# Weight sums of a Strassen-Winograd layer: six slabs in heads 0 to 6, their copies begun by GpSimd

## The chip, the cores and the metric

The kernel is one program on one core of a Trainium2 chip. The metric is the device time of one execution in microseconds (us). The shown time is the median of three runs.

## The reference, cut to what matters

One decoder layer over 512 tokens of width 2048, in float32. A combined projection feeds two branches of eight heads each, a gated delta rule and block attention. Their outputs are projected up, gated, summed, projected by `w_o` and added to the input.

```python
h = rms_norm(x, norm_w)                       # 512 x 2048
proj = h @ w_in                               # heads' q, k, v, z of both branches, and the gates
oa = gated_delta_rule(...) ; ob = moba_attention(...)
y_gdn, y_moba = oa @ w_out_gdn, ob @ w_out_moba
merged = sigmoid(g_gdn) * y_gdn + sigmoid(g_moba) * y_moba
out = x + merged @ w_o
```

## The kernel before

**Stages.** First the input is normalised and transposed. Then eight heads follow (`head(h, p)` on every engine; heads 1 to 6 are a loop). A head multiplies eight windows of `w_in`, each a block of 2048 x 128 weights (1 MB), with the tokens: the "windows" w = 0 to 7, named `win(w, ...)` on TensorE (PE). Between their pieces TensorE does the small products of the delta rule of head h and of the attention of the head before, p. After the heads come ten "quads", `q` = 0 to 9: 0 to 3 form the gates, 4 to 7 the two up-projections, 8 and 9 the product with `w_o`. A quad is a product of 2 x 2 blocks done with seven block products instead of eight (P11, P12, PS1, PS2, PS4, PS3, P22), each split in units, and for that sums of weight blocks are needed.

**A weight's way.** The sync engine (SP) loads window w into one of four slots (`load`, line 547), once the window that used the slot is done. ScalarE (ACT) rounds it (`split`, line 1386), VectorE (DVE) forms the rest (line 1840), and TensorE multiplies three times (lines 885 to 889). ACT and DVE do this in the order written: a weight that is late holds whatever stands behind its split. In the order of ACT, behind the split of window 1 stand the gate of z, the rounded rotary outputs and the evacuation of window 0 (line 1418); behind the split of window 2 stands the SiLU of head h (lines 1394 to 1398), which leads over DVE lines 1883 and 1887 to TensorE's line 935.

**Weight sums.** `w_out_gdn`, `w_out_moba` and `w_o` need four sums of blocks each, T1 to T4. They are built in DRAM (`weight_sums`) by DMAs alone, in eight slabs of rows, one slab for each head. A slab has 64, 64 and 128 rows of the three weights. It takes 12 plain copies, issued by SP between its weight loads (`sum_copies`, line 554; one or two behind each load), six accumulating DMAs from the weights (`sums_13`, lines 764 and 766), three that add T3 to T2 (`sums_2`, line 772) and three that add T2 to T4 (`sums_4`, line 779). The accumulating ones are issued by GpSimd (POOL), for the slab of the head before. The slabs of heads 6 and 7 are summed by GpSimd in quads 1 and 2, between its stores of the gates. The sums are read from quad 4 on.

**GpSimd's order in a head.** It makes the decay parts (lines 747 to 758), loads the next decay row (742), stores the attention output of the head before (795), issues `sums_13`, does the rotary product of k (`k_rope`, 811), issues `sums_2`, does the rotary product of q (`q_rope`, 811), stores the delta rule's output (815) and issues `sums_4`.

**GpSimd's order in a gate quad.** `add_22` (line 839) adds a weight block to an operand, and `finish_block` (line 847) stores a block of gates to DRAM. ACT may overwrite a block buffer (`e_block`, line 1724) only once its store has landed. Between these stand, in quads 1 and 2:

```python
                for i in range(3):
                    finish_block(q, i)
                    if q in (1, 2):
                        (sums_13, sums_2, sums_4)[i](last - 2 + q)
```

Of the kernel before, what the change touches and what calls it, by code (L numbers as in the profile page):

```python
# [18 lines left out]
H = 8  # L19
# [16 lines left out]
NW = len(STRIPES)  # L36
# [6 lines left out]
COLS = 512  # L43
# [36 lines left out]
def ended(q, p):  # L80
    return unit(q, p, ku(q) - 1) + 1
# [113 lines left out]
T_FIRST = ((0, 0), (0, 0), (0, 1), (1, 0))  # L195
T_OF = {PS1: T1, PS2: T2, PS3: T3, P22: T4}
NT_COPIES = 12
PAIRED = P // 2

(HC_G, HC_CG, HC_B, HC_NB, HC_NBE, HC_KD, HC_GL) = range(7)  # L200
NHC = 7
RING = 4
# [23 lines left out]
def hybrid_layer(nc, x, norm_w, w_in, gdn_conv_w, gdn_a_log, gdn_dt_bias, gdn_norm_w, moba_q_norm_w,  # L226
# [11 lines left out]
    t_dram = [nc.dram_tensor(f"weight_sums{i}", (4, rows, 2, COLS), F32, kind="Internal").ap()  # L238
              for i, rows in enumerate((D // 4, D // 4, D // 2))]
    w_blocks = [w[0].rearrange("(b r) (q s c) -> b r q s c", b=2, q=2, s=2) for w in (w_out_gdn, w_out_moba, w_o)]  # L240
# [3 lines left out]
    with ctx:  # L244
        def sb(name, shape, dt=F32, at=ctx):
            return at.enter_context(nc.sbuf_tensor(name, shape, dt))

        s = {n: ctx.enter_context(nc.semaphore(n)) for n in SEMS}
# [66 lines left out]
        masked4 = sb("masked4", [P, P], at=area)  # L315
        pairs4 = sb("pairs", [P, 4, PAIRED], at=area)
        steps = sb("level_rows", [P, PAIRED], at=area)
        area.close()
# [63 lines left out]
        def compact(ap, rows):  # L382

            return ap[:rows, :NT * PAIRED]

# [89 lines left out]
        def weight_sum(q, t, j):  # L475

            of, at = (2, q - W0) if q >= W0 else ((q - Y0) // 2, q % 2)
            return t_dram[of][t, UK * j * P:UK * (j + 1) * P, at, :].rearrange("(k p) c -> p k c", p=P)

        def slab(of, t, i):  # L480

            r = t_dram[of].shape[1] // H
            return t_dram[of][t, bass.ds(i * r, r), :, :]

        def block_slab(of, kb, cb, i):

            r = t_dram[of].shape[1] // H
            return w_blocks[of][kb, bass.ds(i * r, r), :, cb, :]

        residual = ops[:, SLOT_C, 2, :].rearrange("p (t c) -> p t c", t=2)  # L490

# [35 lines left out]
        def _(sp):  # L527
# [19 lines left out]
                sp.dma_start(raw[slot][:].rearrange("p (k c) -> p k c", k=src.shape[1]), src)\  # L547
                    .then_inc(loaded[slot], 16)

            def sum_copies(i, w):  # L550

                for c in range(w, NT_COPIES, NW):
                    of, t = c % 3, c // 3
                    sp.dma_start(slab(of, t, i), block_slab(of, *T_FIRST[t], i)).then_inc(s["wt_copied"], 16)

            def head_loads(i):
                sp.wait_ge(s["wt_copied"], 16 * NT_COPIES * i)
                for w, (_, col) in enumerate(STRIPES):
                    if w == 0:
                        slot_free(i * NW + 1)  # L560
                    elif w > 1:
                        slot_free(i * NW + w)
                    load(i * NW + w, w % RING, w_in3[:, :, bass.ds(i * P + col, P)])
                    sum_copies(i, w)

            load(0, 0, w_in3[:, :, STRIPES[0][1]:STRIPES[0][1] + P])
            sp.wait_ge(s["sets"], 1)
# [11 lines left out]
            for w in range(RING, NW):  # L579
                slot_free(w)  # L580
                load(w, w % RING, w_in3[:, :, STRIPES[w][1]:STRIPES[w][1] + P])
                for c in range(w - RING, NW, RING):
                    sum_copies(0, c)
            with sp.Fori(1, H) as i:
                head_loads(i)

# [81 lines left out]
            def stream():  # L668

                gate_after = {}  # L670
                for b in range(GATES, 4 * (W0 - Y0)):
                    q, i = Y0 + (b - GATES) // 4, (b - GATES) % 4
                    gate_after[ended(q, BLOCK_PRODUCT[i]) + LEAD + NSTREAM] = (Y0 + b // 4, b % 4)
                sp.wait_ge(s["wt_sums"], 16 * NT_COPIES * H)
                for n in range(unit(Y0), N_UNITS):
                    if n == unit(Y0) + NSTREAM - 1:
                        sp.wait_ge(s["pe_unit"], ended(Y0 - 1, PS4))
                        sp.wait_ge(s["ob_out"], 16 * H)
                        sp.dma_start(stage(1), o_dram[H:].rearrange("k p t -> p k t")).then_inc(s["stage_b"], 16)
                    load_streamed(n)  # L680
                    if n == unit(Y0) + NSTREAM:
                        for b in range(GATES):
                            load_gate(Y0, b)
                    if n in gate_after:
                        load_gate(*gate_after[n])
# [30 lines left out]
        def _(pool):  # L716
# [27 lines left out]
            def decay_parts(h):  # L744
# [12 lines left out]
                pool.wait_ge(s["cg_dts"], 4 * h + 2)  # L757
                pool.tensor_tensor(dTb[:], dTb[:], nb_row, ALU.mult).then_inc(s["cg_dts"], 1)

            def sums_13(i):  # L760

                pool.wait_ge(s["wt_copied"], 16 * NT_COPIES * (i + 1))
                for of in range(3):
                    pool.dma_start(slab(of, T3, i), block_slab(of, 1, 1, i), accum_op=ALU.add).then_inc(s["wt_sums"], 16)
                for of in range(3):
                    pool.dma_start(slab(of, T1, i), block_slab(of, 0, 1, i), accum_op=ALU.add).then_inc(s["wt_sums"], 16)

            def sums_2(i):

                pool.wait_ge(s["wt_sums"], 16 * (NT_COPIES * i + 6))  # L770
                for of in range(3):
                    pool.dma_start(slab(of, T2, i), slab(of, T3, i), accum_op=ALU.add,
                                   max_dma_last_dim=4 * 2 * COLS).then_inc(s["wt_sums"], 16)

            def sums_4(i):

                pool.wait_ge(s["wt_sums"], 16 * (NT_COPIES * i + 9))
                for of in range(3):
                    pool.dma_start(slab(of, T4, i), slab(of, T2, i), accum_op=ALU.add,
                                   max_dma_last_dim=4 * 2 * COLS).then_inc(s["wt_sums"], 16)  # L780

            def head(h, p):

                decay_parts(h)
                if p is None:
                    store_rows()
                if h is not last:
                    decay_row(h + 1)
                if h is last:
                    store_own(0, 0)  # L790
                    store_own(0, 1)
                    store_own(1, 0)
                if p is not None:
                    pool.wait_ge(s["ob"], h)
                    pool.dma_start(o_dram[bass.ds(p + H, 1)].rearrange("o p t -> p (o t)"), pr1[:])\
                        .then_inc(s["ob_out"], 16)
                    if h is not last:
                        sums_13(p)

                if h is last:  # L800
                    store_own(1, 1)
                    store_own(2, 0)
                    store_own(2, 1)
                pool.wait_ge(s["rope_loaded"], 16)
                for c, r in ((0, kr), (1, qr)):
                    if h is last and c == 1:
                        store_own(3, 0)
                        store_own(3, 1)
                    pool.wait_ge(s["b_n"], 2 * h + c + 1)
                    pool.wait_ge(s["s_mm"], 4 * h)  # L810
                    pool.tensor_tensor(r[:], pt[:, c, :], cos, ALU.mult).then_inc(s["b_cos"], 1)
                    if c == 0 and p is not None and h is not last:
                        sums_2(p)
                pool.wait_ge(s["o_2"], h + 1)
                pool.dma_start(o_dram[bass.ds(h, 1)].rearrange("o p t -> p (o t)"), o1[:]).then_inc(s["o_out"], 16)
                if p is not None and h is not last:
                    sums_4(p)

            last = H - 1
# [4 lines left out]
                pool.wait_ge(s["a_step"], own_count(OWN_LAST[i], half))  # L824
                pool.dma_start(own_dram[i][:, k], own[:, k]).then_inc(own_stored[half], 16)

            head(0, None)
            with pool.Fori(1, H - 1) as i:
                head(i, i - 1)
            head(last, last - 1)  # L830

# [29 lines left out]
            for q in range(NQ):  # L862
                if q < Y0:
                    add_22(q, 0)
                    add_22(q, 1)
                if q > 0:
                    finish_block(q - 1, 3)
                if q < Y0:
                    add_22(q, 2)
                    add_22(q, 3)  # L870
                for i in range(3):
                    finish_block(q, i)
                    if q in (1, 2):
                        (sums_13, sums_2, sums_4)[i](last - 2 + q)
            for i in range(4):
                pool.wait_ge(e_stored[i], stored(LAST if i < 3 else LAST - 1))

# [2 lines left out]
        def _(pe):  # L880
# [92 lines left out]
            def ma(h, k):  # L973
# [6 lines left out]
                if k == NL - 1:  # L980
                    for t in range(NT):
                        mm = pe.matmul(G0[:LAST_ROWS, t * PAIRED:(t + 1) * PAIRED], Ln[:, t * P:t * P + LAST_ROWS],
                                       xa[:, tile4h(t)[1]], start=True, stop=True)
                else:
                    m = P - b
                    for t in range(NT):
                        mm = pe.matmul(G0[:m, t * PAIRED:(t + 1) * PAIRED], Ln[:, t * P:t * P + m],  # L987
                                       half_tile(xa, t, b, 1), start=True, stop=True)
# [1589 lines left out]
```

## Time and profile before

| | us |
|---|---|
| median of 3 runs | 1577.79 |
| lowest, highest | 1574.37, 1577.83 |
| the profiled execution's own time | 1578.1 |
| its span in the profile | 1576.5 |
| TensorE busy | 1535.1 (97%) |
| VectorE, ScalarE, GpSimd busy | 1064.0, 766.4, 251.4 |

The profile lists busy time by engine, what ended each idle stretch, and the DMA queues: the queue `hardware_dynamic` takes what SP issues, `software_dynamic` what GpSimd issues. An engine that is rarely idle bounds the kernel; idle time elsewhere costs nothing by itself. Timelines give each instruction's start and length in us, and in brackets the idle time before it and what ended it. TensorE's instructions overlap, so its pace is read from the distance of their starts.

### The profile page before, as it was taken

To read this page: it belongs to the slowest core of one execution; us is meant where nothing else is said; L and a number is where in the kernel's file an instruction comes from. 1 tells how busy PE (TensorE), PEld (TensorE's weight loads), DVE (VectorE), ACT (ScalarE), POOL (GpSimd) and SP (SyncE) were. 2 spreads that over 40 slices of the span, in tenths; PEclk is the share of its full clock that TensorE was granted. 3 is DMA by queue.
4 is the path that set the end of the run, shared out by engine and by line. 5 is a ranking of instruction groups with operands and counts; after the bars stand their busy time and mean duration, and the time that the engine had idled before them with its cause. 6 is when DMAs were issued, how large, how long until landed. Compare 5 with 4: busy or idle time off the path is not lost.

```text
span 1576.5 us, 20948 instructions
## 1 busy us (share of the span) xinstructions
PE 1535.1 (97%) x7591; PEld 1285.3 (82%) x7591; DVE 1064.0 (67%) x1331; ACT 766.4 (49%) x1007; POOL 251.4 (16%) x253
## 2 busy tenths in 40 slices
PE   6999999999999999999999999999797999999998
PEld 5888888888888888888888888887686888888887
DVE  6665756746757557657578879685674898767744
ACT  5434434335344344344344456655473775556542
POOL 4202023023112121140230101112021000100000
PEclk9999999999999999999999999999898999999999
DMA  8426369288376575493593467679598688986864
GB/s 271 142 87 201 106 123 258 75 183 222 95 194 175 121 191 168 99 245 114 108 257 115 147 233 179 193 236 248 139 254 194 224 281 306 310 258 206 255 207 107
DMA packets 236320, 296.74 MB, mean 188 GB/s; under 512 B 11299, under 2 KB 143654, under 8 KB 235174
## 3 DMA queue, kind: packets, MB, share of 16 engines
q1 hardware_dynamic: 208006, 221.46, 44.8%
q0 software_dynamic: 28256, 74.49, 22.5%
q8 instruction: 37, 0.61, 0.2%
q14 instruction: 21, 0.17, 0.0%
HBM read 270.72 MB, written 96.50 MB: 233 GB/s over the span
## 4 chain that ended last, share of the span: by engine, by line
PE 88%; DMA 7%; DVE 2%; ACT 1%; POOL 1%; issue 1%; SPq 0%; ACTq 0%; DVEq 0%
PE bank L885 15%; PE bank L889 15%; PE bank L887 14%; PE bank L1326 10%; PE bank L1328 10%; PE bank L1330 10%; DMA weight_sums<-in_w_o_dram 3%; PE bank L914 2%; DMA gates<-e_block 2%; PE bank L987 1%; PE bank L1004 1%; DMA weight_sums<-weight_sums 1%; PE bank L1081 1%; PE bank L919 1%; DMA x_tiles<-in_x_dram 1%
## 5 line engine op out<-in xcount | busy, mean ns | idle before, releaser
L885 PE MATMUL bank<-h_hi_r,w_hi 128*128 128x512 f32 x1008 | 407.4, 404 | 0.0
L889 PE MATMUL bank<-h_hi_r,w_raw_r 128*128 128x512 f32 x1008 | 394.6, 391 | 0.0
L887 PE MATMUL bank<-h_lo_r,w_hi 128*128 128x512 f32 x1008 | 393.6, 390 | 0.0
L2341 DVE TENSOR_TENSOR ring_lo<-operands,ring_hi 128x1024 fp32r<-128x1024 f32 x224 | 271.1, 1221 | 166.6 <-ACT ring_hi L1683 165.0
L1683 ACT ACTIVATE ring_hi<-operands 128x1024 fp32r<-128x1024 f32 x224 | 235.3, 1059 | 209.5 <-PE bank L1330 190.6
L889 PEld LDWEIGHTS bank<-h_hi_r,w_raw_r 128*128 128x128 f32 x1008 | 189.2, 188 | 41.5
L887 PEld LDWEIGHTS bank<-h_lo_r,w_hi 128*128 128x128 f32 x1008 | 189.9, 188 | 34.7
L885 PEld LDWEIGHTS bank<-h_hi_r,w_hi 128*128 128x128 f32 x1008 | 189.8, 188 | 34.1
L1326 PE MATMUL bank<-ring_hi,h_hi_r 128*128 128x512 f32 x480 | 188.5, 393 | 0.2 <-issue 0.2
L1328 PE MATMUL bank<-ring_lo,h_hi_r 128*128 128x512 f32 x480 | 186.8, 389 | 0.0
L1840 DVE TENSOR_TENSOR w_raw_r<-w_raw,w_hi 128x2048 fp32r<-128x2048 f32 x64 | 151.2, 2363 | 32.1 <-ACT w_hi L1386 31.0
L1330 PE MATMUL bank<-ring_hi,h_lo_r 128*128 128x512 f32 x416 | 161.9, 389 | 0.0
L1330 PE MATMUL bank<-ring_hi,sums_r 128*128 128x512 f32 x384 | 151.5, 394 | 0.0
L1326 PE MATMUL bank<-ring_hi,sums_r 128*128 128x512 f32 x320 | 127.8, 399 | 20.6 <-DVE ring_lo L2341 20.6
L1328 PE MATMUL bank<-ring_lo,sums_r 128*128 128x512 f32 x320 | 126.7, 396 | 0.0
L1386 ACT ACTIVATE w_hi<-w_raw 128x2048 fp32r<-128x2048 f32 x64 | 122.1, 1908 | 0.0
L1326 PEld LDWEIGHTS bank<-ring_hi,h_hi_r 128*128 128x128 f32 x480 | 90.1, 188 | 19.4 <-issue 0.8
L1328 PEld LDWEIGHTS bank<-ring_lo,h_hi_r 128*128 128x128 f32 x480 | 90.1, 188 | 18.7 <-issue 0.2
L1330 PEld LDWEIGHTS bank<-ring_hi,h_lo_r 128*128 128x128 f32 x416 | 78.1, 188 | 16.3
L1326 PEld LDWEIGHTS bank<-ring_hi,sums_r 128*128 128x128 f32 x320 | 61.4, 192 | 34.8 <-issue 21.1
L1330 PEld LDWEIGHTS bank<-ring_hi,sums_r 128*128 128x128 f32 x384 | 73.4, 191 | 15.7
L1328 PEld LDWEIGHTS bank<-ring_lo,sums_r 128*128 128x128 f32 x320 | 61.5, 192 | 12.7
(327 smaller groups left out, 2172.0 us busy)
## 6 DMA issues: line engine op xcount, KB each, us to landing
w_raw<-in_w_in_dram SPq DMA_DIRECT2D x64, 1024.0 KB, 7.5
operands<-in_w_in_dram SPq DMA_DIRECT2D x64, 512.0 KB, 5.7
operands<-weight_sums SPq DMA_DIRECT2D x64, 512.0 KB, 5.3
weight_sums<-in_w_o_dram SPq DMA_DIRECT2D x32, 512.0 KB, 6.2
operands<-in_w_o_dram SPq DMA_DIRECT2D x24, 512.0 KB, 5.0
weight_sums<-in_w_out_gdn_dram SPq DMA_DIRECT2D x32, 256.0 KB, 6.3
weight_sums<-in_w_out_moba_dram SPq DMA_DIRECT2D x32, 256.0 KB, 7.5
weight_sums<-in_w_o_dram POOLq DMA_DIRECT2D x16, 512.0 KB, 13.5
```

The lines of the kernel that those rows point to most:

```text
L885: pe.matmul(PJ[slot % 2][:], w_hi[slot % 2][:, c], h_hi[:, k, :], start=(k == 0), stop=False, skip_group_check=True)
L887: pe.matmul(PJ[slot % 2][:], w_hi[slot % 2][:, c], h_lo[:, k, :], start=False, stop=False, skip_group_check=True)
L889: mm = pe.matmul(PJ[slot % 2][:], w_lo[slot][:, c], h_hi[:, k, :], start=False, stop=(k == KT - 1), skip_group_check=True)
L914: mm = pe.matmul(ps[:, tile4(t)], lhsT[:, tile4(t)], rhs[:, tile4(t)], start=True, stop=True)
L919: mm = pe.transpose(ps[:, tile4(t)], src[:, tile4(t)], ident[:])
L1326: pe.matmul(ps[:], a_hi, ring_hi[:, n % RINGS, c], start=(FRESH[p] and k == 0), stop=False, skip_group_check=True)
L1328: pe.matmul(ps[:], a_hi, ring_lo[:, n % RINGS, c], start=False, stop=False, skip_group_check=True)
L1330: mm = pe.matmul(ps[:], a_lo, ring_hi[:, n % RINGS, c], start=False, stop=(k == kn - 1), skip_group_check=True)
L1386: act.activation(w_hi[slot % 2][:], raw[slot][:], ACT.Copy).then_inc(s["hi_ready"], 1)
L1683: act.activation(ring_hi[:, n % RINGS, :], operand(q, p, j), ACT.Copy).then_inc(s["op_hi"], 1)
L1840: dve.tensor_tensor(w_lo[slot][:], raw[slot][:], w_hi[slot % 2][:].bitcast(F32), ALU.subtract)\
L2341: dve.tensor_tensor(ring_lo[:, n % RINGS, :], operand(q, p, j), ring_hi[:, n % RINGS, :].bitcast(F32), ALU.subtract).then_inc(s["op_lo"], 1)
```

## The change

The sums are built in six slabs instead of eight. Each but the last has 88, 88 and 176 rows; the last (slab 5) has 72, 72 and 144. The twelve copies of slab i are issued by GpSimd in head i, for i = 0 to 5: six behind the rotary product of k (and behind `sums_2`, where there is one), six behind the rotary product of q. SP issues no copies and no longer waits for them at a head's start. `sums_13`, `sums_2` and `sums_4` of slab i are issued in head i + 1, so all is done in heads 0 to 6; quads 1 and 2 have no sums. The accumulating DMAs between sums are cut into pieces of half the length.

```diff
+SLABS = H - 2
+LAST_SLAB = SLABS - 1
...
+        def slab_rows(of, i):
+
+            n = t_dram[of].shape[1]
+            r = 8 * -(-n // (8 * SLABS))
+            if i is LAST_SLAB:
+                return slice(i * r, n)
+            return bass.ds(i * r, r)
...
-            def sum_copies(i, w):
-
-                for c in range(w, NT_COPIES, NW):
-                    of, t = c % 3, c // 3
-                    sp.dma_start(slab(of, t, i), block_slab(of, *T_FIRST[t], i)).then_inc(s["wt_copied"], 16)
...
             def head_loads(i):
-                sp.wait_ge(s["wt_copied"], 16 * NT_COPIES * i)
...
                     load(i * NW + w, w % RING, w_in3[:, :, bass.ds(i * P + col, P)])
-                    sum_copies(i, w)
...
+            def sum_copies(i, first):
+
+                for t in (first, first + 1):
+                    for of in range(3):
+                        pool.dma_start(slab(of, t, i), block_slab(of, *T_FIRST[t], i)).then_inc(s["wt_copied"], 16)
...
-                                   max_dma_last_dim=4 * 2 * COLS).then_inc(s["wt_sums"], 16)
+                                   max_dma_last_dim=2 * 2 * COLS).then_inc(s["wt_sums"], 16)
...
-            def head(h, p):
+            def head(h, p, copied=None):
...
                     if c == 0 and p is not None and h is not last:
                         sums_2(p)
+                    if copied is not None:
+                        sum_copies(copied, 2 * c)
...
-            head(0, None)
-            with pool.Fori(1, H - 1) as i:
-                head(i, i - 1)
+            head(0, None, 0)
+            with pool.Fori(1, LAST_SLAB) as i:
+                head(i, i - 1, i)
+            head(LAST_SLAB, LAST_SLAB - 1, LAST_SLAB)
+            head(SLABS, LAST_SLAB)
             head(last, last - 1)
...
-                    if q in (1, 2):
-                        (sums_13, sums_2, sums_4)[i](last - 2 + q)
```

## Rows read from the trace of the kernel before

**Rows 1.** The page: busy time by engine, and its share.
```profile
PE 1535.1 (97%) x7591; PEld 1285.3 (82%) x7591; DVE 1064.0 (67%) x1331; ACT 766.4 (49%) x1007; POOL 251.4 (16%) x253
```

**Rows 2.** Windows: one head, quad 1, quad 3; granted clock, DMA share, GB/s last.
```profile
501.00:612.00 111.00, 111.00 (x582) 93.75 (x581) 70.13 (x106) 48.07 (x72) 22.26 (x21) 1.00 0.64 161
1048.00:1138.00 90.00, 79.61 (x340) 65.30 (x339) 55.01 (x53) 45.48 (x49) 17.73 (x20) 0.92 0.82 212
1228.00:1315.00 87.00, 87.00 (x386) 72.03 (x385) 75.11 (x76) 62.32 (x70) 4.36 (x8) 1.00 0.82 284
```

**Rows 3.** Chain of work across the end of quad 1: start, us, what.
```profile
1083.27 9.81 DMA weight_sums<-weight_sums
...
1096.41 12.90 DMA gates<-e_block
```

**Rows 4.** TensorE's timeline at the starts of quads 2 and 3.
```profile
1112.82 0.76 PE L1326 MATMUL bank<-ring_hi,sums_r 128*128 128x512 f32 x1 [10.39 <-DVE ring_lo L2341]
...
1118.93 0.40 PE L1330 MATMUL bank<-ring_hi,sums_r 128*128 128x512 f32 x1
1119.16 0.40 PE L1326 MATMUL bank<-ring_hi,sums_r 128*128 128x512 f32 x1
...
1201.99 0.77 PE L1326 MATMUL bank<-ring_hi,sums_r 128*128 128x512 f32 x1 [9.88 <-DVE ring_lo L2341]
```

**Rows 5.** ScalarE's timeline at the start of quad 1.
```profile
1022.02 1.09 ACT L1724 ACTIVATE e_block<-bank 128x512 f32<-128x512 f32 x2 [5.52 <-DMA gates<-e_block]
```

**Rows 6.** GpSimd's timeline, end of head 4 and start of head 5.
```profile
560.95 2.44 POOL L772 DMA_DIRECT2D weight_sums<-weight_sums  x3
578.86 1.79 POOL L811 TENSOR_TENSOR q_rope<-pt,cossin 128x512 f32<-128x512 f32 x1 [15.46 <-DVE pt L2031]
...
588.46 1.04 POOL L747 TENSOR_TENSOR lower<-lower,hcol 128x512 f32<-128x512 f32 x1 [1.24 <-ACT lower L1434]
```

**Rows 7.** The sync engine's timeline there: the loads of windows 0 and 2.
```profile
564.01 0.38 SPq L547 DMA_DIRECT2D w_raw<-in_w_in_dram  x1
...
577.54 0.38 SPq L547 DMA_DIRECT2D w_raw<-in_w_in_dram  x1
```

**Rows 8.** DMA issues: the loads issued at 564.01, 625.42 and 646.00; last is us to landing.
```profile
w_raw<-in_w_in_dram SPq DMA_DIRECT2D x1, 1024.0 KB, 9.5
...
w_raw<-in_w_in_dram SPq DMA_DIRECT2D x1, 1024.0 KB, 6.2
...
w_raw<-in_w_in_dram SPq DMA_DIRECT2D x1, 1024.0 KB, 13.9
```

**Rows 9.** DMA queues, 652 to 656: packets, MB, share of 16 engines.
```profile
q0 software_dynamic: 355, 0.66, 89.3%
q1 hardware_dynamic: 358, 0.19, 22.9%
```

**Rows 10.** DMA packets in 628 to 631, 674 to 678, and 683 to 685.
```profile
DMA packets 1632, 0.95 MB, mean 316 GB/s; under 512 B 17, under 2 KB 1554, under 8 KB 1632
...
DMA packets 217, 0.76 MB, mean 189 GB/s; under 512 B 32, under 2 KB 32, under 8 KB 217
...
DMA packets 675, 0.77 MB, mean 385 GB/s; under 512 B 31, under 2 KB 389, under 8 KB 675
```

**Rows 11.** ScalarE's timeline, the splits of windows 0, 1 and 2 of head 5.
```profile
581.15 1.90 ACT L1386 ACTIVATE w_hi<-w_raw 128x2048 fp32r<-128x2048 f32 x1
...
589.25 1.91 ACT L1386 ACTIVATE w_hi<-w_raw 128x2048 fp32r<-128x2048 f32 x1
...
600.13 1.91 ACT L1386 ACTIVATE w_hi<-w_raw 128x2048 fp32r<-128x2048 f32 x1
```

**Rows 12.** VectorE's timeline behind the split of window 2.
```profile
603.98 2.29 DVE L1840 TENSOR_TENSOR w_raw_r<-w_raw,w_hi 128x2048 fp32r<-128x2048 f32 x1
...
608.29 0.69 DVE L1887 TENSOR_TENSOR raw_gk_r<-raw_gk,out_norm_r 128x512 fp32r<-128x512 f32 x1 [1.42 <-ACT out_norm_r L1447]
```

**Rows 13.** TensorE's timeline, the product that waits for it.
```profile
612.36 0.39 PE L935 MATMUL bank<-out_norm_r,ones 128*128 128x512 f32 x1
```

More of the change, by code:

```diff
@@ L478, in weight_sum @@
             return t_dram[of][t, UK * j * P:UK * (j + 1) * P, at, :].rearrange("(k p) c -> p k c", p=P)
+        def slab_rows(of, i):
[4 more added lines that the diff above has]
+            return bass.ds(i * r, r)
         def slab(of, t, i):
-            r = t_dram[of].shape[1] // H
-            return t_dram[of][t, bass.ds(i * r, r), :, :]
+            return t_dram[of][t, slab_rows(of, i), :, :]
         def block_slab(of, kb, cb, i):
-            r = t_dram[of].shape[1] // H
-            return w_blocks[of][kb, bass.ds(i * r, r), :, cb, :]
+            return w_blocks[of][kb, slab_rows(of, i), :, cb, :]
         residual = ops[:, SLOT_C, 2, :].rearrange("p (t c) -> p t c", t=2)
@@ L581, in _ @@
                 load(w, w % RING, w_in3[:, :, STRIPES[w][1]:STRIPES[w][1] + P])
-                for c in range(w - RING, NW, RING):
-                    sum_copies(0, c)
             with sp.Fori(1, H) as i:
@@ L673, in stream @@
                     gate_after[ended(q, BLOCK_PRODUCT[i]) + LEAD + NSTREAM] = (Y0 + b // 4, b % 4)
-                sp.wait_ge(s["wt_sums"], 16 * NT_COPIES * H)
+                sp.wait_ge(s["wt_sums"], 16 * NT_COPIES * SLABS)
                 for n in range(unit(Y0), N_UNITS):
@@ L779, in sums_4 @@
                     pool.dma_start(slab(of, T4, i), slab(of, T2, i), accum_op=ALU.add,
-                                   max_dma_last_dim=4 * 2 * COLS).then_inc(s["wt_sums"], 16)
-            def head(h, p):
+                                   max_dma_last_dim=2 * 2 * COLS).then_inc(s["wt_sums"], 16)
+            def head(h, p, copied=None):
                 decay_parts(h)
```

## The prediction

> **What bounds the kernel now.** First the page: TensorE is busy for 97% of the span [rows 1], so only what makes it wait, run at a lower clock or do other work counts; the change leaves its work alone. Then the windows by stage: in the head stage TensorE is never idle, with the DMA engines busy for 0.64 of the time; in quad 3 it is never idle either; in quad 1 it is busy for 79.6 of 90 us and its mean clock is 0.92 [rows 2]. Quad 2 repeats quad 1.
>
> Then TensorE's timeline: it stands still for 10.39 us where quad 2 begins and for 9.88 us where quad 3 begins [rows 4]. The chain of work says for what: GpSimd waits for a DMA between sums (9.81 us), then stores the last gates of the quad, and this store takes 12.90 us to land [rows 3]; only then may ScalarE empty the bank. So the stalls come from sums standing in GpSimd's order ahead of a gate store, and from their bytes in the same DMA engines. After a stall the distance of matmul starts is 0.43 us and not 0.23: the 14 steps from 1112.82 to 1118.93 take 6.11 us instead of 3.2 [rows 4], the 1.2 GHz level instead of the 2.4.
>
> **What the removal in quads 1 and 2 gives.** Idle 10.39 + 9.88 = 20.3 us, plus 2.9 us of low clock twice, is 26 us. What is late next: the same store without sums ahead of it. The trace has this case at the start of quad 1: ScalarE waits 5.52 us for the gates, until 1022.02 [rows 5], and TensorE does not wait. Shifted by a quad (76.2 us, which is 336 matmuls of 0.227) this gives 1098.2 for the start of quad 2, against 1109.4 now, 11.2 us earlier and so 0.8 more than the stall: just enough. I take the full 26 us; the lower bound is half of it, if one of the two stays.
>
> **What the heads pay: GpSimd's order.** Three DMAs hold GpSimd for 2.44 us [rows 6], so six copies take 4.9. Those behind k's product and `sums_2` end near 568.5; q's product starts at 578.86 after 15.46 us idle [rows 6], so 10 us are spare. Those behind q's product end near 585.6; behind them wait the store of the delta rule's output (0.6 us), `sums_4` (2.4) and the decay parts, which start at 588.46 now [rows 6] and then near 588.7 or a us later. VectorE reads them behind its line 1887, at 608.29 [rows 12], when they have been done for over 10 us. Price nothing. SP loses waits that hid nothing: its loads start when a slot is free [rows 7].
>
> **What the heads pay: the DMA engines.** Now a copy stands in SP's queue behind a load and can't delay it. Then the copies are in GpSimd's queue, beside the loads. From 652 to 656 both queues had work, a load beside accumulating sums, and moved 355 and 358 packets [rows 9]: they take turns packet by packet, though one's are 2 KB and the other's 512 B. That load took 13.9 us to land, one alone 6.2 [rows 8]. (By the Trainium skill, DMA: Bandwidth & Descriptors, Queues, rings and completion order, each engine goes round the queues packet by packet; the trace agrees.)
>
> Price of a packet on one of 16 engines: a load's 512 B, 48 / 1632 = 0.03 us; a 4 KB piece of `sums_2`, 64 / 185 = 0.346; a copy's 2 KB, by 385 GB/s over 16, 0.085 [rows 10]. A GpSimd copy is not in the trace. Its bounds are 0.07 (the same window, loads taken out) and 0.161 (an accumulating 2 KB packet, 64 x 0.893 / 355 [rows 9]). I take 0.085, since SP's plain copies are of the same blocks.
>
> Per engine a load has 128 packets, `sums_2` 22 (16 x 1.375), each half of the copies 2 x (11 + 11 + 22) = 88, `sums_4` 22. Walk through the end of head 4 with the times of [rows 6, 7], a first packet 1.6 us after an issue (4 for GpSimd's copies, an estimate) and 0.6 from the last packet to landing:
> - Load 0, issued 564.01, starts at 565.6. `sums_2` has 13 packets left: 13 x 0.376 = 4.9, to 570.5. Then 88 turns of 0.115 beside copies, 10.1, to 580.6; 27 left alone, 0.8. Lands 582.0 (now 573.5 [rows 8]).
> - Load 1, queued behind, runs alone until the second six copies begin at 584.7, then 18 turns beside them. Lands 587.4.
> - Load 2, issued 577.54, meets 70 copies (8.1 us, to 594.9), the store (0.8) and all of `sums_4` (22 x 0.376 = 8.3, to 604.0), then 32 alone. Lands 605.6 instead of about 585.
>
> The limits. TensorE reaches window 2 nine matmuls before 612.36 [rows 13], so at 610.3, window 1 at 599.4, window 0 at 588.5. A weight needs 1.9 us of ScalarE [rows 11] and 2.3 of VectorE [rows 12] first. So load 0 must land by 584.3, load 1 by 594.5, load 2 by 606.1. Behind the split of window 2 stands one more thing: line 1887 ends at 608.98 [rows 12], 3.4 us before its product at 612.36 [rows 13]; VectorE's split may begin at 607.4 instead of 603.98, so load 2 must land by 605.5. By the walk it is 0.1 us late, with nothing to spare. Slabs of 88 rows don't divide by 16, so some engines carry more than 88 packets; each extra one costs 0.115, and a load lands with its last engine. I add 1.4 us: 1.5 us lost in a head.
>
> This meets the heads that have `sums_2`, copies and `sums_4`, 1 to 5: 5 x 1.5 = 7.5 us. In head 0 there are no sums (15 us less traffic): nothing. Head 6 has sums alone: nothing. `sums_13` grows from 64 to 88 packets, 24 x 0.161 = 4 us, beside the load of window 7, which has 20 us of cover: nothing.
>
> **Sum.** 1578.1 - 26 + 7.5 = 1559.6 on the profiled execution, whose own time is 0.3 above the median: 1559.5.
>
> **Rivals.**
> - *The loads come too late (slower).* Place: load 1 and load 2 at a head's start. Both sets of 88 copies lie ahead of load 2, so each 0.01 us on a copy's packet costs 1.8 us a head. From 0.114 us a packet on, the loss passes 26 / 5 = 5.2 us a head and the kernel is slower. At 0.13, load 2 is 8 us late, 40 in all: 1592. At 0.161, load 0 lands at 588.7 and load 1, which meets all 88 later copies and `sums_4`, at 615, 20 us late: 1650. For it: turns by packet, the DMA share of 0.64 over a whole head already [rows 2]. Against it: SP's copies at 385 GB/s. Chance 0.22.
> - *Uneven engines.* If the 88-row transfers all lie on the same eleven engines, those carry 108 copies and 32 pieces of sums: 2 x (20 x 0.115 + 10 x 0.376) = 12 us later for load 2, 1612. The Trainium skill (same page, Why a DMA increments its semaphore by 16 and not by 1) says that a DMA uses the largest number up to 16 that divides its slowest dimension, 11 for 88 rows, from a cursor that moves on for GpSimd's. No row here shows a size that doesn't divide by 16. With the cursor the excess is a few packets, which my 1.4 us covers. Its chance is within the 0.22.
> - *No price at all.* A packet at 0.07 lands load 2 at 603: 1552. Chance 0.10.
> - *The gain is only moved.* The gate stores of quads 1 and 2 stay late by DMA load alone, and one stall remains: 1572. Against it: quad 3, as loaded with DMA (0.82) and never idle [rows 2]. Chance 0.05.
> - *GpSimd blocks* on copies that find no room behind queued ones, until they drain at 581: q's product 2 us late, then VectorE and its split of window 0, which has 3 us spare. With it the time is above 1565. Chance 0.03.
>
> **How the numbers follow.** My forecast, 0 to 4 us lost a head, 1553 to 1573, has 0.54; no price 0.10; slower 0.22; what is left, 0.06, is a loss near 5 us a head, no change. A measurement of this kernel tells about 0.3%, 4.7 us. The moved gain and the block end faster. Faster 0.71, same 0.07, slower 0.22. The range reaches from the case of no price, 1551, into the slow rival, 1600, leaving out what lies beyond a packet of 0.14; the likeliest case's own is 1553 to 1573.
>
> **What would show it.** Right: no wait of TensorE above 1 us at the starts of quads 2 and 3, clock 1.00 in quad 1, gate stores landing in 7 to 9 us; in the heads, the loads of windows 0, 1 and 2 landing near 18, 23 and 28 us after issue, q's product and the decay parts on time; TensorE idle 0 to 4 us about 24 us into a head (line 935 or window 2). Wrong: loads landing in 8 to 10 us (then the queues share otherwise than by turns), TensorE idle at windows 0 or 1 of a head, a period of a head above 116 us with lower clock behind the stall, or copies' packets at other than 0.07 to 0.1 us.

## The result, and the profile after

| | before | after |
|---|---|---|
| median of 6 runs, us | 1575.86 | 1615.24 |
| lowest, highest | 1574.37, 1577.83 | 1610.74, 1618.6 |
| span of the profiled execution | 1576.5 | 1617.0 |
| TensorE busy | 1535.1 | 1542.0 |

The ratio is 1.0246, 95% interval 1.0225 to 1.0268: slower, where 1559.5 and faster had been forecast. It is outside the range (1551 to 1600) too. Ratios, here and below, compare undisturbed executions alone; one of E10 (5492 us) and one of E12 (2194 us), far off all others, are in no ratio, but the medians listed for these two runs count them.

The page of the kernel after: busy time by engine, granted clock in 40 slices, and the loads (the last figure is the median us to landing).

```profile
PE 1542.0 (95%) x7591; PEld 1289.2 (80%) x7591; DVE 1055.3 (65%) x1331; ACT 765.5 (47%) x1007; POOL 264.8 (16%) x301
...
PEclk9999998998998998999999999999999999999999
...
w_raw<-in_w_in_dram SPq DMA_DIRECT2D x64, 1024.0 KB, 9.7
```

The list of TensorE's waits: us in all, times, the longest. L889 is the first product of every window, so its line adds the waits of all windows.

```profile
PE bank L889 <- DVE w_raw_r L1844: 54.3, 6, 12.5
PE bank L1258 <- DVE x_tiles L2243: 11.1, 1, 11.1
PE bank L1330 <- DVE ring_lo L2345: 0.8, 1, 0.8
```

Windows of the kernel after: the end of head 4, the 12.5 us behind its stall, and quad 1; clock, DMA share, GB/s last [rows 2].

```profile
533.00:644.50 111.50, 100.03 (x533) 84.33 (x532) 62.80 (x100) 41.50 (x63) 22.38 (x28) 0.97 0.64 160
644.50:657.00 12.50, 12.50 (x49) 10.22 (x50) 5.25 (x6) 6.00 (x9) 5.45 (x5) 0.88 0.95 253
1079.00:1166.00 87.00, 87.00 (x386) 72.04 (x385) 58.71 (x56) 50.06 (x54) 12.49 (x13) 1.00 0.72 214
```

The quads are as forecast: no stall left that counts, clock 1.00 in quad 1, where it was 0.92 [rows 2, 4]. The time was lost in the heads, where the forecast had lost 1.5 us each. TensorE's timeline has a stall at the start of each of heads 2 to 6, at the first product of window 0 (the sixth wait of L889, 1.6 us, is at window 1 of head 6):

```profile
267.37 0.79 PE L889 MATMUL bank<-h_hi_r,w_hi 128*128 128x512 f32 x1 [11.61 <-DVE w_raw_r L1844]
...
393.06 0.79 PE L889 MATMUL bank<-h_hi_r,w_hi 128*128 128x512 f32 x1 [12.26 <-DVE w_raw_r L1844]
...
519.24 0.79 PE L889 MATMUL bank<-h_hi_r,w_hi 128*128 128x512 f32 x1 [12.45 <-DVE w_raw_r L1844]
...
644.47 0.79 PE L889 MATMUL bank<-h_hi_r,w_hi 128*128 128x512 f32 x1 [11.47 <-DVE w_raw_r L1844]
645.06 0.63 PE L891 MATMUL bank<-h_lo_r,w_hi 128*128 128x512 f32 x1
645.49 0.63 PE L893 MATMUL bank<-h_hi_r,w_raw_r 128*128 128x512 f32 x1
...
762.01 0.79 PE L889 MATMUL bank<-h_hi_r,w_hi 128*128 128x512 f32 x1 [4.87 <-DVE w_raw_r L1844]
```

Behind a stall the starts are 0.43 us apart, the 1.2 GHz level, as behind the stalls of the quads before [rows 4].

Back from there: ScalarE's split of window 0 waited for the load. Timeline of ScalarE in the kernel after:

```profile
640.10 1.91 ACT L1390 ACTIVATE w_hi<-w_raw 128x2048 fp32r<-128x2048 f32 x1 [14.58 <-DMA w_raw<-in_w_in_dram]
```

And GpSimd's timeline there, 44.3 us later than in the trace before because of the earlier stalls (the load of window 0 is issued at 608.27 and not at 564.01 [rows 7]):

```profile
605.22 2.71 POOL L774 DMA_DIRECT2D weight_sums<-weight_sums  x3
606.94 1.56 POOL L760 DMA_DIRECT2D weight_sums<-in_w_out_gdn_dram  x1
...
624.88 0.57 POOL L760 DMA_DIRECT2D weight_sums<-in_w_out_gdn_dram  x1
```

The DMA issues of the kernel after: the load issued at 608.27, and the mean of the two (windows 0 and 1) issued from 608 on:

```profile
w_raw<-in_w_in_dram SPq DMA_DIRECT2D x1, 1024.0 KB, 31.8
...
w_raw<-in_w_in_dram SPq DMA_DIRECT2D x2, 1024.0 KB, 36.3
```

So load 0 (window 0's) took 31.8 us, load 1 40.9, and load 2 27.7. It was 9.5 for load 0 before [rows 8], and the walk had 18, 23 and 28. Load 2, at which the walk put the loss, takes what was forecast from its issue on, but it is issued late: SP's instruction for load 1 lasts 16.8 us, from 608.8 to 625.6, and load 2 follows it at 625.9 instead of 621.8. The loads issued by SP at 608.8 and 625.9; durations in ns:

```profile
L553 SPq DMA_DIRECT2D w_raw<-in_w_in_dram x2: 16814/17803/18792, 608.8 to 625.9; - x2
```

Set back by the 44.3 us, the three loads land at 595.8, 605.4 and 609.3 on the clock of the trace before, against the prediction's limits of 584.3, 594.5 and 605.5. So all three are late: by 11.5, 10.9 and 3.8 us. TensorE shows the first alone, because its stall of 11.5 us moves the limits of the other two. That nobody waits for load 2 therefore doesn't say that it came in time.

The DMA queues of the kernel after, in 608 to 612, 617 to 620, 626 to 628 and 628 to 630: packets, MB, share of 16 engines (q0 is GpSimd's, q1 SP's).

```profile
q0 software_dynamic: 343, 0.64, 105.6%
...
q0 software_dynamic: 295, 1.01, 87.2%
q1 hardware_dynamic: 297, 0.15, 17.8%
...
q0 software_dynamic: 97, 0.35, 53.7%
q1 hardware_dynamic: 387, 0.20, 32.3%
...
q1 hardware_dynamic: 640, 0.33, 73.7%
q0 software_dynamic: 58, 0.17, 29.1%
```

Three things are to be seen. For 3.7 us after its issue the load moved nothing. Beside the copies it moved packet for packet (295 to 297), 0.15 MB against 1.01. (By the Trainium skill, DMA: Bandwidth & Descriptors, Queues, rings and completion order, each engine serves the queues in turn by packet; the trace agrees.) And the first six copies run out at 626 to 628, just as the second six, issued from 624.88 with some 4 us to their first packet, come in.

### The profile page after: what moved, and what is told of

It reads as the page before. It is cut to its first block, busy times and chain, and to the rows that moved or that the text cites. A ratio compares the mean times of both kernels' runs of the same rounds, so it can differ in the third digit from the quotient of the medians.

```text
span 1617.0 us, 20695 instructions
## 1 busy us (share of the span) xinstructions
PE 1542.0 (95%) x7591; PEld 1289.2 (80%) x7591; DVE 1055.3 (65%) x1331; ACT 765.5 (47%) x1007; POOL 264.8 (16%) x301
## 4 chain that ended last, share of the span: by engine, by line
PE 84%; DMA 12%; DVE 3%; ACT 1%; issue 1%; SPq 0%; ACTq 0%; DVEq 0%
PE bank L889 12%; PE bank L1330 12%; PE bank L1332 12%; PE bank L1334 12%; PE bank L893 12%; PE bank L891 12%; DMA w_raw<-in_w_in_dram 10%; PE bank L918 2%; PE bank L991 1%; PE bank L1008 1%; PE bank L1085 1%; DVE w_raw_r L1844 1%; PE bank L923 1%; ACT w_hi L1390 1%; DMA x_tiles<-in_x_dram 1%
## 5 line engine op out<-in xcount | busy, mean ns | idle before, releaser
L889 PE MATMUL bank<-h_hi_r,w_hi 128*128 128x512 f32 x1008 | 413.2, 410 | 54.3 <-DVE w_raw_r L1844 54.3
L893 PE MATMUL bank<-h_hi_r,w_raw_r 128*128 128x512 f32 x1008 | 398.6, 395 | 0.0
L891 PE MATMUL bank<-h_lo_r,w_hi 128*128 128x512 f32 x1008 | 398.0, 395 | 0.0
L889 PEld LDWEIGHTS bank<-h_hi_r,w_hi 128*128 128x128 f32 x1008 | 192.8, 191 | 91.7 <-issue 54.7
L1334 PE MATMUL bank<-ring_hi,sums_r 128*128 128x512 f32 x384 | 149.5, 389 | 0.0
L1330 PE MATMUL bank<-ring_hi,sums_r 128*128 128x512 f32 x320 | 125.1, 391 | 0.8 <-DVE ring_lo L2345 0.8
L1332 PEld LDWEIGHTS bank<-ring_lo,sums_r 128*128 128x128 f32 x320 | 60.1, 188 | 12.3
```

The lines of the kernel that those rows point to most:

```text
L889: pe.matmul(PJ[slot % 2][:], w_hi[slot % 2][:, c], h_hi[:, k, :], start=(k == 0), stop=False, skip_group_check=True)
L891: pe.matmul(PJ[slot % 2][:], w_hi[slot % 2][:, c], h_lo[:, k, :], start=False, stop=False, skip_group_check=True)
L893: mm = pe.matmul(PJ[slot % 2][:], w_lo[slot][:, c], h_hi[:, k, :], start=False, stop=(k == KT - 1), skip_group_check=True)
L1330: pe.matmul(ps[:], a_hi, ring_hi[:, n % RINGS, c], start=(FRESH[p] and k == 0), stop=False, skip_group_check=True)
L1332: pe.matmul(ps[:], a_hi, ring_lo[:, n % RINGS, c], start=False, stop=False, skip_group_check=True)
L1334: mm = pe.matmul(ps[:], a_lo, ring_hi[:, n % RINGS, c], start=False, stop=(k == kn - 1), skip_group_check=True)
```

## The experiments

Runs of one batch shared their runs of the kernel before: 1576.13 us in the first (E1, E2, E4, E6), 1576.03 in the second (E3, E7a, E7b, E8), 1576.81 in the third (E10, E12) and 1576.05 in the fourth (E13, E14).

| run | time, us | ratio to before | TensorE's waits for a window's weight: us, times |
|---|---|---|---|
| the change | 1615.2 | 1.0246 | 54.3, 6 |
| E1 rows divide by 16 | 1620.5 | 1.0277 [1.0257, 1.0297] | 57.6, 6 |
| E2 sums in long pieces | 1621.3 | 1.0292 [1.0246, 1.0339] | 55.5, 9 |
| E6 both | 1622.6 | 1.0292 [1.0268, 1.0316] | 64.5, 5 |
| E4 eight slabs, GpSimd copies | 1577.7 | 1.0012 [1.0002, 1.0021] | none |
| E3 six slabs, SP copies | 1551.2 | 0.9838 [0.9818, 0.9858] | none |
| E7a first six copies away | 1551.8 | 0.984 [0.9819, 0.9862] | none |
| E7b second six away | 1580.6 | 1.0032 [1.0009, 1.0054] | 22.5, 5 |
| E8 copies timed by windows | 1551.2 | 0.9836 [0.9816, 0.9856] | none |
| E10 second six behind load 0 | 1569.3 (four of its runs: 1562.2 to 1569.9) | 0.9939 [0.9917, 0.9961] | 7.3, 5 |
| E12 load 0 a window earlier | 1568.6 | 0.9943 [0.9925, 0.9962] | 10.4, 6 |
| E13 E10 with rows of E1 | 1576.1 | 1.0003 [0.9991, 1.0015] | 14.5, 4 |
| E14 sums_2 cut short | 1553.2 | 0.9852 [0.9836, 0.9869] | 2.2, 1 |

The last column is of the profiled execution, all windows together. In the change, E1, E6, E7b, E10 and E13 at least nine tenths of it stand at window 0. In E2 it is 21.9 us at window 0 and 33.6 at window 1; in E12 and E14 all of it stands at windows 1 and 2.

### Is it the shape of the slabs or of the pieces? (E1, E2, E6)

```diff
# E1 (and E6)
-            r = 8 * -(-n // (8 * SLABS))
+            r = 32 * -(-n // (32 * SLABS))
# E2 (and E6), in sums_2 and sums_4
-                                   max_dma_last_dim=2 * 2 * COLS)
+                                   max_dma_last_dim=4 * 2 * COLS)
```

> The changed kernel, but with slabs of 96, 96 and 192 rows (the last 32, 32, 64) instead of 88, 88 and 176 (72, 72, 144), so that every transfer divides evenly over 16 engines; the short pieces of the accumulating DMAs stay. The changed kernel took 1615 us, 12 us of idle at the start of each of five heads, in front of window 0. 
> The changed kernel with the accumulating DMAs between sums cut into pieces as long as before (16 KB instead of 8 KB); the 88-row slabs stay. The trace of the changed kernel shows these sums as 2 KB packets at 0.21 us, those of before as 4 KB packets at 0.346. Theory 'turns': half as many turns for the same bytes, 22 fewer for load 0 and 22 fewer for load 2, each of 0.04 to 0.2 us: the wait at window 0 shrinks from 12 to 5 to 8 us, 1580 to 1597. Theory 'uneven engines': the packets ahead of a load on the fullest engine are still 1.45 times the mean, so the wait stays at 9 to 12 us, 1600 to 1615.

> Both: slabs of 96, 96, 192 rows and the long pieces. This is what the forecast's walk assumed (even load, sums in 4 KB packets). By it: load 0 lands near 18 us, load 2 near 30 us after issue, 0 to 3 us lost a head: 1553 to 1568. If it stays above 1590, neither unevenness nor piece length is the cause, and the copies' place in the second queue alone is ('issuer').

Neither, as far as the time goes. E1 kept the stall at window 0, and E6, with 96 rows and the pieces as before the change, had the longest. Its waits of TensorE:

```profile
PE bank L889 <- DVE w_raw_r L1844: 64.5, 5, 20.3
```

96 rows are 9% more bytes in each of the first five slabs, and the loads of windows 0 and 1 took 37.3 and 46.0 us. The rival of uneven engines, in the form in which the prediction had it, falls. E1's time lies outside the ranges of both its theories.

E2 says more than its time. With half as many turns in the sums, load 0 lands after 21.3, 35.4, 20.8, 22.6 and 23.4 us at the ends of heads 1 to 5: in four of five near its limit of 20.3, as the theory of turns expected. But load 1 still takes 39.3 to 44.0 us, and the wait moves to window 1. ScalarE's timeline in E2, its splits of windows 0 and 1 of head 5, behind which TensorE waits 2.3 and 7.0 us:

```profile
631.91 1.92 ACT L1390 ACTIVATE w_hi<-w_raw 128x2048 fp32r<-128x2048 f32 x1 [5.37 <-DMA w_raw<-in_w_in_dram]
651.75 1.91 ACT L1390 ACTIVATE w_hi<-w_raw 128x2048 fp32r<-128x2048 f32 x1 [12.31 <-DMA w_raw<-in_w_in_dram]
```

So load 0 in time is not enough. In these four heads the two waits together are 8 to 13 us, most of it at window 1, and the time is 1621 against an expectation of 1580 to 1597.

### Is it GpSimd as the issuer, or six slabs? (E4, E3)

```diff
# E4, against the kernel before: SP's sum_copies taken out, and in GpSimd's head()
+                    sum_copies(h, 2 * c)
# E3, against the changed kernel: GpSimd's taken out, and in SP's head_loads()
+                    if copied:
+                        sum_copies(i, w)
```

> Only the issuer is changed: eight slabs of 64, 64, 128 rows as before, slabs 6 and 7 summed in quads 1 and 2 as before, pieces long as before, but the copies of slab h are issued by GpSimd behind the rotary products of head h, in all eight heads. By the walk with 64 copies' and 16 sums' packets of a third less: load 0 lands near 578, load 1 and 2 by 587: no loss in the heads, and the two stalls of 10 us stay: 1573 to 1583. Rival 'issuer' (copies in GpSimd's queue hold the loads whatever their size): 5 to 10 us a head in seven heads, 1610 to 1650.

> Six slabs of 88 rows as in the changed kernel, sums in heads 0 to 6, short pieces, but the copies issued by SP behind its loads as before. It measures the gain of quads 1 and 2 alone, with whatever longer slabs cost in SP's own queue. Theory (both): the two stalls of 10 us and their low clock are gone and nothing is lost in the heads, 1550 to 1557. If it stays above 1565, the gain was over-sized, or 88-row slabs cost something whoever issues them.

Each part alone costs nothing in the heads; the rival that E6 had left, the issuer alone, falls with E4. With eight slabs of 64 rows and GpSimd as issuer, loads 0, 1 and 2 land after 16.5, 19.2 and 21.3 us, all in time. With six slabs and SP as issuer, load 0 lands after 12.8 and load 2 after 8.2. Together they cost 64 us. E3 also measures the other part of the change alone: 1.62% of 1576, 25.5 us, is what the quads give.

### Which of the two sets of copies? (E7a, E7b, E8)

```diff
# E7a: behind sums_13, instead of behind k's product (E7b: 2, instead of behind q's)
+                if copied is not None:
+                    sum_copies(copied, 0)
# E8: copies begun by the windows done, behind decay_row (those behind the rotary products taken out)
+                    for first in (0, 2):
+                        pool.wait_ge(s["win_done"], h * NW + 2 + first // 2)
+                        sum_copies(copied, first)
# E8: the copies now run a head ahead of sums_13
-                pool.wait_ge(s["wt_copied"], 16 * NT_COPIES * (i + 1))
+                pool.wait_ge(s["wt_copied"], 16 * NT_COPIES * (i + 1 if i is LAST_SLAB else i + 2))
```

> The changed kernel, but the first six copies are issued 25 us earlier, behind the six accumulating DMAs that follow the store of the attention output; the second six stay behind q's product. Theory 'second six on an unfinished load' (the load of window 0 waits behind sums and copies until the second six begin, and then takes turns with those too): with the first six gone, load 0 meets only the three sums and lands in 10 to 13 us, load 1 before the second six; load 2 alone meets them, 20 to 27 us: no wait of TensorE over 2 us, 1552 to 1562. Rival 'second six alone' (they hold load 2 and with it the head): 5 to 8 us a head stay, 1575 to 1595.

> The mirror of it: the first six stay behind k's product, the second six are issued 30 us earlier, behind the six accumulating DMAs. Theory 'second six on an unfinished load': sums and first six drain near 584, load 0 is done 1 to 3 us later (20 to 22 us after its issue instead of 32), on the edge of its limit of 584.3 + 0 to 3 us; load 1 and 2 then run free: 0 to 3 us a head, 1552 to 1568. Rival 'first six alone' (sums and six copies ahead of load 0 are enough): 10 us and more stay, 1600 and above.

> Six slabs, copies by GpSimd, but issued where the DMA engines are idle: the first six once windows 0 and 1 of the head are done, the second six once window 2 is done, ahead of the store of the attention output. The loads issued there have 35 us and more of cover. Every theory that puts the loss on the loads of windows 0 to 2 expects no loss in the heads and the full gain in the quads: 1549 to 1555. If not, the loss lies with GpSimd's order or the number of copies.

The second six alone (E7a) cost nothing; the first six alone (E7b) cost 22.5 us of stalls, unevenly. ScalarE's timeline in E7b, its splits of window 0 in two heads:

```profile
252.98 1.92 ACT L1392 ACTIVATE w_hi<-w_raw 128x2048 fp32r<-128x2048 f32 x1 [4.43 <-DMA w_raw<-in_w_in_dram]
...
369.52 1.91 ACT L1392 ACTIVATE w_hi<-w_raw 128x2048 fp32r<-128x2048 f32 x1 [8.44 <-DMA w_raw<-in_w_in_dram]
```

These loads landed 21.7 and 25.7 us after issue, with 20.3 to spend. The time, 1580.6, lies between what the theory (1552 to 1568) and its rival (1600 and more) expected. Half of the 22.5 us is one head: there load 0 took 32.2 us though no second set was near. What came in before it was through were the store and `sums_4`, issued from 482.5 on and landed from 487 to 497; load 0, issued at 462.48, landed at 494.7. So the next batch need not be copies. Both sets together cost more than the sum of each alone: 54.3 against 22.5 + 0.

### Does the second set meet an unfinished load? (E10, E14, E12, E13)

```diff
# E10
                     if copied is not None:
+                        if c == 1:
+                            pool.wait_ge(s["raw_loaded0"], (2 * h + 3) * 16)
                         sum_copies(copied, 2 * c)
# E14, in sums_2
-                    pool.dma_start(slab(of, T2, i), slab(of, T3, i), accum_op=ALU.add,
+                    pool.dma_start(slab(of, T2, i)[0:16], slab(of, T3, i)[0:16], accum_op=ALU.add,
# E12, at the end of SP's head_loads (the load of w == 0 at its start is taken out)
+                if i is not LAST_HEAD:
+                    slot_free(i * NW + NW)
+                    load(NW, 0, w_in3[:, :, bass.ds(i * P + P + STRIPES[0][1], P)])
```

E13 is E10 with the line of E1.

> The changed kernel, but GpSimd begins the second six copies of a head only when the load of the next head's window 0 has landed. Theory (the first six are almost through when the second six begin, and load 0 then takes turns with all of the second six): load 0 ends 1 to 3 us after the first six, lands 20 to 24 us after its issue instead of 31.8, TensorE waits 0 to 6 us a head instead of 12, and the time is 1551 to 1585, near the run with the second six moved away (1580.6) or below it. Rival (the first six and sums_2 alone make load 0 late, the second six only add bytes to the loads behind it): load 0 still lands after 27 us or more, TensorE waits 10 us or more a head, and the time is 1605 or more.

> The changed kernel with the twelve copies of a head where they are; of each DMA of the second sum (sums_2) only the first 16 rows are added and the others are left out, which takes away some 20 of 22 packets of an engine ahead of the first copies. Theory (the first six copies and load 0 end just too late for the second six; 4 to 5 us less ahead of them clears it): load 0 lands 17 to 22 us after its issue, TensorE waits under 3 us a head, 1551 to 1565. Rival (two sets of copies within a load's cover are too much by themselves): load 0 lands after 27 us or more, TensorE waits 8 us or more a head, 1590 or more.

> The changed kernel with its copies where they are, but SP issues the load of the next head's window 0 one window earlier, as soon as its slot is free, and not together with that of window 1. Theory (only load 0 is late, because it alone lies beside both sets of copies with 20 us of cover): load 0 lands some 15 us earlier and is never waited for; load 1, which now starts where load 0 did, has 10 us more cover; loads 1 and 2 still meet copies and cost 0 to 4 us a head: 1551 to 1572. Rival (the whole stretch is short of DMA bandwidth, so that the wait passes to the next load): TensorE waits 8 us or more a head at window 1 or 2, and the time is 1590 or more.

> The run in which GpSimd waits for load 0, with slabs of 96 rows and a last one of 32, which divide by 16. In the run with 88 rows a load's worth of packets (2048) had passed about 3.5 us before load 0 landed, 21.8 us after its issue: the last engine is behind the mean one. Theory (rows that don't divide by 16 put some engines behind): load 0 lands within 1 us of the 2048th packet, 18 to 20 us after its issue, and the time falls to 1552 to 1562. Rival (the last engine is behind for another reason): the landing stays at 21 us or later, the time at 1562 or more.

E10 keeps all bytes and all transfers, and only lets the second six begin behind load 0's landing. The load, issued at 572.24, then lands after 21.9 us, ten earlier. Its row of the DMA issues, then GpSimd's timeline where it waits for the landing:

```profile
w_raw<-in_w_in_dram SPq DMA_DIRECT2D x1, 1024.0 KB, 21.9
```
```profile
594.83 0.57 POOL L760 DMA_DIRECT2D weight_sums<-in_w_out_gdn_dram  x1 [5.94 <-DMA w_raw<-in_w_in_dram]
```

And ScalarE's:

```profile
594.13 1.92 ACT L1392 ACTIVATE w_hi<-w_raw 128x2048 fp32r<-128x2048 f32 x1 [4.63 <-DMA w_raw<-in_w_in_dram]
```

GpSimd waited only 5.94 us: that little separates 1615 from 1562 (the profiled execution of E10). E14 leaves the order alone and takes sums from ahead of the first copies, by leaving out all but the first 16 rows of each DMA of `sums_2`; load 0 lands after 15.0 us and one stall of 2.2 us is left. E12 gives load 0 a window more. Load 1, issued alone at 576.78, 3 us behind `sums_2`, now stands where load 0 stood; its row of the DMA issues:

```profile
w_raw<-in_w_in_dram SPq DMA_DIRECT2D x1, 1024.0 KB, 30.1
```

It is as slow as load 0 was, but has about 10 us more before it is needed, so 10.4 us of stalls stay instead of 54.3. All three times fall where the theory had them (E14's load is 2 us quicker than expected).

The traces show the meeting itself. Each load raises its semaphore 16 times, the last time when it has landed. The table takes these for the landings of its 16 parts, one on each DMA engine; us from the load's issue, at the end of head 4.

| | 1st | 8th | 14th | 15th | last |
|---|---|---|---|---|---|
| before, load 0 | 8.3 | 8.8 | 9.4 | 9.4 | 9.5 |
| the change, load 0 | 17.2 | 18.3 | 20.5 | 26.2 | 31.8 |
| the change, load 1 | 29.9 | 33.2 | 39.3 | 39.5 | 40.9 |
| E10, load 0 | 17.1 | 18.8 | 20.8 | 21.0 | 21.9 |
| E10, load 1 | 20.1 | 21.5 | 23.3 | 23.5 | 24.3 |

Fourteen parts of load 0 land as they do in E10. In the change the last two do not get through before the second set comes (its copies are issued from 16.6 us on; in E10, where they are issued from 594.83 on, none moves before 598.0), and they pay for it with 5 and 10 us. Load 1, which is queued behind load 0, pays on all engines: its first part lands 10 us later than in E10 and its last 17.

E13 went against the theory, by both of its numbers: load 0 lands after 22.7 us, and the time is 1576. Yet there is a gap between mean and last engine. In E10 the queue of the loads had moved a load's 2048 packets by 591 (the DMA queues, 576 to 590 and 590 to 591):

```profile
q1 hardware_dynamic: 1571, 0.80, 22.0%
...
q1 hardware_dynamic: 479, 0.24, 82.5%
```

The load landed at 594.1, 3.1 us later. In E13 the 2048th packet passes just before 603 and it lands at 605.1, 2.1 later. So even rows narrow the gap by a microsecond at most in this head and lose it again to their bytes. By the landings of all five heads they do not narrow it: the last part of load 0 lands 1.6 to 2.7 us behind the mean of the 16 in E10, and 1.4 to 3.2 in E13. (The Trainium skill, DMA: Bandwidth & Descriptors, Why a DMA increments its semaphore by 16 and not by 1, has 88 rows on eleven engines; if this holds here, it isn't what made the load late.)

## Why the prediction was wrong

**The quads: right.** Forecast 26 us; E3, E7a and E8 give 24 to 26 against before. One stall of 0.8 us is left of 20.6. The gate stores land in 2.9 to 7.7 us (forecast 7 to 9), and ScalarE waits for gates at the start of quad 1 as before [rows 5].

**GpSimd's order: right, price nothing.** The twelve copies hold it where it was idle; q's product starts 11.85 us after it is free. In E4 and E8 it issues them all, and no work behind them delays TensorE.

**A copy's price: right.** From 617 to 620, q0's packets took 0.872 x 3 x 16 / 295 = 0.142 us for 3.4 KB, which is 0.042 us a KB; the forecast had 0.085 for 2 KB. The copies go in pieces of up to 4 KB, though, so an engine has about 44 of them in a set and not 88, each a longer turn. The rival of late loads hung on this price (0.114 and more) and named loads 1 and 2. Its sign came true, and so did its mechanism, turns by packet, and load 1 as a place; its condition did not: the loads are late at the forecast price.

**The step that failed: in the walk, load 0 "Lands 582.0", load 1 "Lands 587.4", and the "1.4 us" added for the last engine.** By the forecast load 0's last packet went at 581.4 and the second six came at 584.7, so that load 1 moved most of its packets alone in between and had 18 turns left. The limit for load 0 was 584.3. These margins were taken as safe, and what could be late was priced as a few more turns of 0.115 us. Measured, on the clock of before, load 0 landed at 595.8 and load 1 at 605.4. Four terms use the margins up:

- The first packet 1.6 us after the issue: it is more than 3.7. The trace before already had it: its queues from 564 to 568 show 4 packets of the load issued at 564.01, beside 198 of the sums.

```profile
q0 software_dynamic: 198, 0.68, 99.5%
q1 hardware_dynamic: 4, 0.00, 0.3%
```

- With that, and all of the first set, the 2048th packet passes at 628.4 (1935 from 612 to 628, then 640 in 2 us), which is 584.1 on the clock of before: 2.7 later than forecast, and 0.6 ahead of the second six if these come as forecast. For most engines the walk was nearly right: fourteen parts of load 0 landed at 581.2 to 584.5, forecast 582.0.
- The last engine is some 3 us behind the mean one (E10). Two are not through when the second six come, and what they have left takes turns with them. The load lands at 640.1, 11.7 us after its number of packets had passed, instead of 3.
- With the 2.7 us gone, load 1 has next to nothing of its time alone. All its parts run beside the second six, the last also beside `sums_4`, and land at 594.4 to 605.4 on the clock of before. This needs no slow engine, and E2 shows its price by itself.

One smaller thing was wrong too: SP's loads do not all "start when a slot is free". The issue of load 1 holds SP for 16.8 us, and load 2 starts 4 us late.

So the loss is a step and not a slope: once load 0 meets the second set it is 10 us later (31.8 against 21.9 in E10), and four heads lose 11.5 to 12.5 us and not 1.5. The fifth, where the last slab with its smaller copies is built, loses 6.5. The sum: 54.3 us of stalls, and TensorE busy 12.3 us longer than in E7a (1542.0 against 1529.7), the low clock behind each stall. That is 66.6; the spans differ by 66.0 (1617.0 and 1551.0). Against before, 66 less 25 is the 40 us measured.

Three slips in the prediction's own sums decide nothing. 1559.6 less 0.3 is 1559.3. Load 1's limit, 599.4 less 4.2, is 595.2 and not 594.5. And the rival of uneven engines counts 32 pieces of sums where its own rule for the copies gives 27 (only half of them are of 88 rows), which makes 8 us of its 12.

**What is left open.** Which DMA engines are last, and why, the trace doesn't say, since neither packets nor landings name their engine; rows that divide by 16 don't help. That the unfinished parts take turns with the second set is read from their landings in the change and in E10, not seen packet by packet. The profiled execution of E10 keeps 7.3 us of stalls and is 10 us above that of E7a: load 0 beside the first set and `sums_2` is already 1.6 us over its 20.3 us.

**What beats both.** E3, E7a and E8 are within a microsecond of each other at 1551, 1.6% below the kernel before. The nearest to the change is E7a: six copies behind `sums_13`, six behind q's product.

## What to carry to other kernels

When a bulk transfer moves to another queue, find the last moment at which each load in the old queue must have landed, and what enters the other queue next; a load that is not through by then pays for much or all of the next batch, and so do the loads queued behind it, so a margin of a few microseconds is to be priced as a step, and for the last engine and not the mean one. Hold every load against its own limit, and not only the one that the engine is seen to wait for: the first stall hides the lateness of the next. Take the delay from issue to first packet from a stretch that has the same traffic beside it, not from an idle one. Spread the batches so that each lies in a window of its own: the same bytes then cost nothing (E8).

## What the runs showed of the hardware

- A load issued beside queued sums moved its first packets about 4 us after the issue (before: 4 packets in 564 to 568; after: none in 608.27 to 612, 18 in 612 to 613), while with few sums queued (E14) it moved 525 in the 3.5 us after its issue.
- One megabyte took 6.2 us alone [rows 8]. Beside one set of copies load 0 took 15 to 25.7 us (E14, E4, E10 and E7b), and 32.2 in one head of E7b, where `sums_4` came in before it was through. At the end of head 4 of the change, with two sets, the loads took 27.7 to 40.9.
- In this kernel the queue that a transfer is issued in decides what a load has to take turns with: with the same copies issued by SP behind its loads (E3) load 0 took 12.8 us and load 2 8.2, against 31.8 and 27.7.
- The 16 parts of load 0 landed within 2 us of each other before the change, and within 4.8 us beside a backlog in GpSimd's queue (E10); two stragglers, 5.7 and 11.3 us behind the fourteenth, made the landing of load 0 in the change.
- In the change load 1 is issued 0.6 us behind load 0, and its issue holds SP for 16.8 us; in the kernel before it comes 7 us behind, and holds it for 0.5.
